# Attention heads taken in pairs: scores on both row halves of TensorE, products with V on both column halves

## What is computed

```python
def latent_attention(q, k, v, kc, vc):
    kk = jnp.concatenate([k, kc], axis=1)
    vv = jnp.concatenate([v, vc], axis=1)
    ...
    def block(qblk):
        s = jnp.einsum('bqkgd,bmkd->bkgqm', qblk, kk).astype(jnp.float32) * scale
        p = jax.nn.softmax(s, axis=-1).astype(vv.dtype)
        return jnp.einsum('bkgqm,bmkd->bqkgd', p, vv)
def token_mixer(...):
    att = latent_attention(q, k, heads(av, ATT_KV_HEADS), kc, vc)
```

## Time and profile before

| | us |
|---|---|
| time, median of 3 runs (3872.47 to 3875.03) | 3874.95 |
| the profiled execution, its own time | 3873.86 |
| its span from first to last instruction | 3872.1 |
| TensorE busy | 3644.5 (94%) |
| VectorE busy | 2787.8 (72%) |
| ScalarE busy | 2025.3 (52%) |
| granted TensorE clock, mean | 0.978 |

### The profile page before, as it was taken

One profiled execution on the slowest core, in us unless ns is written; L12 is line 12 of the kernel. 1 busy time (PEld: TensorE's weight loads), 2 busy tenths in 40 slices (PEclk: granted clock), 3 DMA queues, 4 the chain that ended last, 5 costly groups with the idle time before them and its releaser, 6 DMA issues.

```text
span 3872.1 us, 60781 instructions
## 1 busy us (share of the span) xinstructions
PE 3644.5 (94%) x22550; PEld 3149.5 (81%) x22550; DVE 2787.8 (72%) x5634; ACT 2025.3 (52%) x4198; POOL 0.2 (0%) x4
## 2 busy tenths in 40 slices
PE   7999999999997999999997999989899999969998
PEld 5876787788876899999996788878698888858887
DVE  5446744499969588888668766674765899697666
ACT  3344422466667555555557544445354666674443
POOL 0000000000000000000000000000000000000000
PEclk9999899999999999999999999999899999999999
DMA  5212223365644565556564466533044565504565
GB/s 204 80 55 99 93 88 103 109 181 183 186 150 137 153 184 185 185 185 187 186 185 131 153 190 190 175 112 106 1 148 138 176 188 181 182 1 152 185 187 159
DMA packets 142196, 568.32 MB, mean 147 GB/s; under 512 B 15808, under 2 KB 17344, under 8 KB 130240
## 3 DMA queue, kind: packets, MB, share of 16 engines
q1 hardware_dynamic: 142016, 566.16, 46.3%
HBM read 565.05 MB, written 1.05 MB: 146 GB/s over the span
## 4 chain that ended last, share of the span: by engine, by line
PE 77%; DVE 19%; ACT 2%; issue 1%; DMA 0%; SPq 0%; DVEq 0%; ACTq 0%
PE ps L530 48%; PE ps L952 12%; DVE arena L1631 11%; PE ps L970 9%; PE ps L954 6%; DVE low L1631 3%; ACT arena L1121 1%; PE ps L744 1%; DVE arena L2123 0%; DVE arena L2114 0%; DVE ring_low L1631 0%; DVE arena L2116 0%; DMA ring<-wmod_in 0%; DVE arena L2111 0%; DVE arena L2120 0%
## 5 line engine op out<-in xcount | busy, mean ns | idle before, releaser
L1121 ACT ACTIVATE high<-ring 128x512 fp32r<-128x512 f32 x1632 | 1028.5, 632 | 1026.9 <-PE ps L530 501.8
L1631 DVE TENSOR_TENSOR low<-ring,high 128x512 fp32r<-128x512 f32 x1632 | 1075.7, 688 | 286.6 <-ACT high L1121 275.8
L530 PE MATMUL ps<-h_pair,high 128*128 128x512 f32 x3456 | 1236.5, 398 | 17.4 <-DVE h_pair L1631 10.1
L530 PE MATMUL ps<-h_pair,low 128*128 128x256 f32 x3456 | 979.2, 283 | 0.0
L530 PEld LDWEIGHTS ps<-h_pair,high 128*128 128x128 f32 x3456 | 653.5, 189 | 171.1 <-issue 11.9
L952 PE MATMUL ps<-wt,high 128*128 128x512 f32 x2048 | 718.5, 397 | 5.7 <-DVE low L1631 5.7
L530 PEld LDWEIGHTS ps<-h_pair,low 128*128 128x128 f32 x3456 | 654.6, 189 | 0.0
L954 PE MATMUL ps<-wt,low 128*128 128x256 f32 x2048 | 572.0, 279 | 0.0
L530 PE MATMUL ps<-arena 128*128 128x128 f32 (+8 forms) x2456 | 408.6, 324 | 135.5 <-ACT arena L1121 109.5
L530 PEld LDWEIGHTS ps<-arena 128*128 128x128 f32 (+2 forms) x2456 | 306.6, 200 | 216.2 <-ACT arena L1121 133.3
L1121 ACT ACTIVATE arena<-ps 128x256 f32<-128x256 f32 (+2 forms) x658 | 273.1, 425 | 395.8 <-PE ps L530 352.1
(11 more groups left out here) (174 smaller groups left out, 4099.8 us busy)
## 6 DMA issues: line engine op xcount, KB each, us to landing
ring<-u_in SPq DMA_DIRECT2D x384, 512.0 KB, 3.5
ring<-v_in SPq DMA_DIRECT2D x384, 512.0 KB, 3.5
ring<-win_in SPq DMA_DIRECT2D x56, 1024.0 KB, 4.9
ring<-wmod_in SPq DMA_DIRECT2D x24, 1024.0 KB, 4.9
ring<-wq_in SPq DMA_DIRECT2D x48, 512.0 KB, 3.6
ring<-wmod_in SPq DMA_DIRECT2D x48, 512.0 KB, 3.7
ring<-wbr_in SPq DMA_DIRECT2D x16, 768.0 KB, 4.2
ring<-wout_in SPq DMA_DIRECT2D x8, 1024.0 KB, 4.9
```

Source lines behind the costliest of these rows:

```text
L530: return pe.matmul(o, l_, r, start=first, stop=last)
L1121: return act.activation(o, i_, f, **kw_)
L1631: return dve.tensor_tensor(o, a, b, op)
```

## The change

Heads are taken in the order 0, 4, 1, 5, 2, 6, 3, 7, so that neighbours in `att` lie on different row halves. TensorE issues the scores of two heads, one behind the other, and then the transposes of two heads. It runs four heads ahead instead of three (`att_p` has 4 buffers, and four scores stand ahead of the `mv` projection). In the products with V, `att_pT[part]` now holds two heads of each half (0, 1, 4, 5 and then 2, 3, 6, 7); for each block of keys there are two matmuls of 256 moving columns, one with the first 64 columns of V into partitions 0 to 63 and one with the other 64 into partitions 64 to 127. The arithmetic is the same, so is the number of scores and transposes. There are 80 matmuls with V of 256 columns in place of 40 of 512. VectorE and ScalarE keep their steps and their order in the list of heads, with each lead longer by one.

```diff
+HEADS = (0, 4, 1, 5, 2, 6, 3, 7)
...
-        att_p = view(s_mlT, 3, T)
+        att_p = view(s_mlT, 4, T)
...
-                def values(t, half):
+                def values(t, part):
...
-                    pe.wait_ge(*at("att_t_read", l, t, 4 * half + 3))
-                    part = slice(half * AD, (half + 1) * AD)
+                    pe.wait_ge(*at("att_t_read", l, t, 5 + 2 * part))
+                    two = slice(part * 2 * P, (part + 1) * 2 * P)
                     for m in range(n_m):
-                        i = mm(out_bank[t][part, :], v_tm[:, m, part],
-                               att_pT[half][:, m, :, :].rearrange("p a b -> p (a b)"), m == 0, m == n_m - 1)
-                    i.then_inc(*inc("att_pv", l, t, half))
+                        for half in range(2):
+                            hp = slice(half * AD, (half + 1) * AD)
+                            i = mm(out_bank[t][hp, two], v_tm[:, m, hp],
+                                   att_pT[part][:, m, 2 * half:2 * half + 2, :].rearrange("p a b -> p (a b)"),
+                                   m == 0, m == n_m - 1)
+                    i.then_inc(*inc("att_pv", l, t, part))
...
-                for s_ in range(3):
+                for s_ in range(4):
                     scores(*att[s_])
                 token_slot(s0 + SLOT_MV[1], "mv", 1, list(range(NT)))
-                turn_p(0, *att[0])
-                for s_, (t, h) in enumerate(att):
-                    if s_ + 3 < len(att):
-                        scores(*att[s_ + 3])
-                    if s_ + 1 < len(att):
-                        turn_p(s_ + 1, *att[s_ + 1])
+                for s_ in range(0, len(att), 2):
+                    t, h = att[s_]
+                    if s_ + 4 < len(att):
+                        scores(*att[s_ + 4])
+                        scores(*att[s_ + 5])
+                    turn_p(s_, *att[s_])
+                    turn_p(s_ + 1, *att[s_ + 1])
                     if h == 0 and t != outs(l)[0]:
                         values(t - 1, 1)
-                    if h == 4:
+                    if h == 2:
                         values(t, 0)
                 values(outs(l)[-1], 1)
...
-                    if i_ >= 3:
-                        act.wait_ge(*at("att_t", l, *att[i_ - 3]))
+                    if i_ >= 4:
+                        act.wait_ge(*at("att_t", l, *att[i_ - 4]))
...
-                    if s_ + 3 < len(att):
-                        weights(s_ + 3, *att[s_ + 3])
+                    if s_ + 4 < len(att):
+                        weights(s_ + 4, *att[s_ + 4])
                     if s_ + 1 < len(att):
                         copy_p(*att[s_ + 1])
...
+                    if s_ + 4 < len(att):
+                        smax(*att[s_ + 4])
                     if s_ + 3 < len(att):
-                        smax(*att[s_ + 3])
-                    if s_ + 2 < len(att):
-                        divide(s_ + 2, *att[s_ + 2])
+                        divide(s_ + 3, *att[s_ + 3])
```

More of the change, by code:

```diff
@@ L726, in _ @@
                 i.then_inc(*inc("cums", l))
-                att = [(t, h) for t in outs(l) for h in range(AH)]
+                att = [(t, h) for t in outs(l) for h in HEADS]
                 def scores(t, h):
@@ L743, in turn_p @@
                     for m in range(n_keys // P):
-                        i = pe.transpose(b[:, m * P:(m + 1) * P], att_p[:, i_ % 3, m * P:(m + 1) * P], ident)
+                        i = pe.transpose(b[:, m * P:(m + 1) * P], att_p[:, i_ % 4, m * P:(m + 1) * P], ident)
                     i.then_inc(*inc("att_t", l, t, h))
-                def values(t, half):
+                def values(t, part):
                     n_m = (T if t >= 2 else SEQ) // P
-                    if half == 0:
+                    if part == 0:
@@ L1321, in weights @@
                     act.wait_ge(*at("att_max", l, t, h))
-                    if i_ >= 3:
-                        act.wait_ge(*at("att_t", l, *att[i_ - 3]))
-                    fn(att_p[:, i_ % 3, 0:n_keys], b[:, 0:n_keys], ACT.Exp, scale=AD ** -0.5,
+                    if i_ >= 4:
+                        act.wait_ge(*at("att_t", l, *att[i_ - 4]))
+                    fn(att_p[:, i_ % 4, 0:n_keys], b[:, 0:n_keys], ACT.Exp, scale=AD ** -0.5,
                        bias=mx[:, t, h:h + 1], accum_out=rsum[:, t, h:h + 1]).then_inc(*inc("att_s_read", l, t, h))
-                for s_ in range(3):
+                for s_ in range(4):
                     weights(s_, *att[s_])
@@ L1342, in copy_p @@
                     n_m = (T if t >= 2 else SEQ) // P
-                    half = h // 4
+                    part, place = h % 4 // 2, h // 4 * 2 + h % 2
                     b = bank("att_t", l, t, h)
-                    if h % 4 == 0 and t != outs(l)[0]:
-                        act.wait_ge(*at("att_pv", l, t - 1, half))
-                    fn(att_pT[half][:, 0:n_m, h % 4, :], b[:, 0:n_m * P].rearrange("p (a b) -> p a b", b=P), ACT.Copy
+                    if h in (0, 2) and t != outs(l)[0]:
+                        act.wait_ge(*at("att_pv", l, t - 1, part))
+                    fn(att_pT[part][:, 0:n_m, place, :], b[:, 0:n_m * P].rearrange("p (a b) -> p a b", b=P), ACT.Copy
                        ).then_inc(*inc("att_t_read", l, t, h))
@@ L1357, in _ @@
                 for s_, (t, h) in enumerate(att):
[L1358 to L1359 removed]
+                    if s_ + 4 < len(att):
+                        weights(s_ + 4, *att[s_ + 4])
                     if s_ + 1 < len(att):
                         copy_p(*att[s_ + 1])
[L1362 removed]
+                    if h == HEADS[2] and t != outs(l)[0]:
                         copy_out(t - 1)
@@ L1816, in divide @@
                     link(dve.reciprocal(rinv[:, t, h:h + 1], rsum[:, t, h:h + 1]))
-                    dve.tensor_scalar(att_p[:, i_ % 3, 0:n_keys], att_p[:, i_ % 3, 0:n_keys], rinv[:, t, h:h + 1], None,
+                    dve.tensor_scalar(att_p[:, i_ % 4, 0:n_keys], att_p[:, i_ % 4, 0:n_keys], rinv[:, t, h:h + 1], None,
                                       ALU.mult).then_inc(*inc("att_n", l, t, h))
-                for s_ in range(3):
+                for s_ in range(4):
                     smax(*att[s_])
```

3 lines of the change are left out of this document (1 added, 2 removed).

## The result

The changed kernel takes 3837.55 us (median of four runs, 3832.38 to 3842.01), the kernel before beside it 3873.71 (3861.88 to 3875.03). The ratio is 0.991, with a 95% interval from 0.989 to 0.992. Five more executions on another occasion gave a median of 3835.3 against 3874.41, ratio 0.990 [0.988, 0.992]. The forecast of 3833 us, with a range from 3826 to 3847, holds.

What follows compares the result with a forecast made beforehand. TensorE was taken to bound the attention; savings of 24.7 us in layer 0, 14.7 in layer 1 and 1.3 ahead of them made 40.7, so 3873.9 - 40.7 = 3833 us. Range 3826 to 3847, to hold 8 in 10.

Steps and rivals of the forecast that it cites:

- The prices: TensorE's attention: 512-key score 1.10 us, paired second score free, four transposes 0.59, eight 1.03, paired products 1.00 and 1.86.
- TensorE's sum: Attention after the change: scores, transposes and products together hold TensorE 37.0 us in layer 0 and 22.3 in layer 1.
- VectorE's pace in tiles 0 and 1: Layer 0, 256 keys: a pair costs VectorE 1.96 us against TensorE's 1.72, adding 8 x 0.24 = 1.9 us.
- tight places: Attention: bank claims while `att_o` is pinned and `copy_out` ahead of an exp add 0.7 us in layer 0, 0.5 in layer 1.
- the end: End of each layer's attention: TensorE waits for the copies of the last two heads, 0.9 us each layer.
- Products not hidden: Attention: VectorE still stands idle while V is multiplied, stages 48 and 28 us, kernel 3845 us; chance 0.12.
- Overlap in part: Attention scores and products: a second tile costs a quarter of its price instead of nothing, 8 us, kernel 3841; chance 0.05.
- none: Attention pairs do not overlap at all; only ways between modes and 3 us of waits go, kernel 3863 us; chance 0.03.
- The clock: Attention falls to 1.2 GHz: over half the new stages, 3858 us, chance 0.05; over both in full, 3882 us, 0.02.
- The signs: Attention some 40 and 24 us, score pairs 0.63 and 1.1, products 1.0 and 1.86, VectorE's score waits below 12, clock 1.00.
- The sign against it: Layer 0's attention: TensorE idle ahead of transposes beyond 4 us would mean VectorE or ScalarE is the bound.
- the likeliest case: Whole kernel: 3833 us, from 3828 without added waits to 3838 with twice as many; chance 0.73.

Runs made afterwards that it cites:

- the run with the short division: Changed kernel with the division touching 2 columns of a head's weights instead of all, so the result is not computed; 3828.93 us.
- the run with the lead alone: Kernel before with four `att_p` buffers and four heads of scores ahead instead of three, all else as it was; 3867.43 us.
- the run with the early transposes: Changed kernel with `copy_out` one head earlier and, in a layer's last tile, the last pair's transposes ahead of the first products; 3835.17 us, ratio 0.990.

## Why the prediction was right

**What bounds the kernel** was read rightly: a microsecond less on TensorE in the attention was one less for the kernel, 38.7 us by the stretches and 36.2 and 39.1 by the two pairs of medians, where the prediction had 40.7.

**The prices.** The score with 512 keys was put at 1.10 from starts of weight loads and is 1.06 from starts of matmuls; the other prices hold within 0.02: 0.63 for a pair with 256 keys, 0.59 and 1.02 for four and eight transposes, 1.0 and 1.88 for the products. The pair on row halves at 512 columns, with bounds of 1.10 and 2.06, is at its lower end.

**TensorE's sum.** 37.0 and 22.3 us forecast, 38.26 and 22.41 busy. Half of what is missing in layer 0 is one pair that did not become one. The weight loads of the third pair of scores in the stretch show it:

```profile
252.44 0.29 PEld L531 LDWEIGHTS ps<-arena 64*128 64x128 f32 x2 [0.17 <-issue]
253.06 0.29 PEld L531 LDWEIGHTS ps<-arena 64*128 64x128 f32 x2 [0.32 <-ACT arena L1126]
```

The second score's load started 0.62 us behind the first's, released by ScalarE, which had still to read its bank, and the pair took 1.24 us instead of 0.63. Here the pair was none because its second wait was met too late; the prediction priced the claims as waits, not as the loss of a partner.

**What is added.** 1.9 for VectorE's pace in tiles 0 and 1, 0.7 for tight places and 0.9 at the end were 3.5 us in layer 0, against 3.95 without work. The run with the short division gives back 1.9 us in layer 0 and 0.1 in layer 1, which agrees with the first in size, but only 1.3 of them come in place, in tiles 0 and 1. The tight places were mis-sized: the claim behind `copy_out`, named as one of them, alone costs 1.16 to 1.25 us, and the prediction did not see that the change moves this copy one head back. The end is 0.64 + 0.74 = 1.38, in both layers, where 0.9 stood: the first of the two, before the last tile's first product, is new. In the kernel before no wait is listed there; two scores of its order stood ahead of that product, where the changed kernel has none left, which is the likely reason and was not tested alone. The forecast for layer 1, 23.7, was 0.3 short, that for layer 0, 40.5, 1.7.

By the rule of the Trainium skill that the emptying of PSUM may become the bound (TensorEngine Tiling (Array Packing), PSUM Bottleneck), VectorE would pace the tiles with 256 keys and, by the rows, just not the others. The runs agree in the main: with the short division layer 0 gained 1.9 us, 1.3 of them in the tiles with 256 keys, and layer 1 gained 0.1.

**The rivals.** *Products not hidden* is out: VectorE's waits fell to 8.0 us, only 1.6 of it outside the stretch of `mv`. It was a good rival, though, since in the run with the lead alone VectorE still waited 24.3 us, so the longer lead was not enough for it. *Overlap in part* and *none* are out by the prices, pair by pair. (*None* was priced with 22 pairs at 0.35 us; the stretches hold 14 + 6 = 20, and the prediction's own prices give 0.14 for the score and 0.15 for the transposes of each, so its 3863 would be some 2 us more. It decides nothing.) By the speedups of TensorE: Matmul & The Clock Gate, Measured speedup vs the span model, in the Trainium skill, which for three and four tiles are below the number of tiles, a second tile might have cost a share of the first; here two tiles did twice the work in 1.00 times the time, in rows (1.06 against 1.06) and in columns (1.88 against 1.87). *The clock* stayed at 2.4 GHz in both attentions, of the changed kernel and of its second execution. The mechanism is real all the same: it struck in the run with the early transposes, for 3.4 us and at a price of 1.5, behind a stretch in which TensorE was busy for 1.73 of 3.41 us, and in the second execution of the kernel before, at a price of 1.6, behind one with 2.82 of 3.42. That it left the two executions of the changed kernel alone is two draws and no more.

**The signs** it named came as written: attention near 40 and 24 us, pairs at 0.63 and 1.06, products at 1.0 and 1.88, waits below 12 us, and clock 1.00. The sign against it, more than 4 us of idle TensorE ahead of transposes in layer 0, did not come: the listed waits there are 1.7 + 0.2 = 1.9 us, and all its idle time is 3.95.

**The range.** 3838 as the upper end of the likeliest case covers the medians, and the range holds them, but the 2 us that it allowed for the rest of the kernel, from three runs 2.6 us apart, were too few. The executions of one kernel lay 10 to 23 us apart. In the profiled ones the stages with two durations make up most of such a spread; the others have no trace. That the medians came so near the sum is in part luck: in and ahead of the attentions the change saved 2.0 us less than forecast, and the medians lay 36.2 us apart on one occasion and 39.1 on the other.

## What to carry to other kernels

Here matmuls that use half the rows or half the columns of the array took no longer in pairs than alone, so count a change to pairs as one price per pair, and then look at what the halves wait for, since a partner that comes late is no partner. Adding up a short stretch of the trace from single prices, with the pace of the next engine beside it, gave the saving within 6%; what was missed were claims on banks at the seams between tiles, one of them made by a small move of a copy in the change itself. And an experiment that is to take an overlap away must put something between the two halves that can't overlap: changing the order of the code left most of it in place.

## What the runs showed of the chip that was not expected

- TensorE starts a matmul of the other column half while three records are still ahead of it in order. Sixteen records of two halves took 1.88 us in alternation, 1.93 in groups of four, and 2.79 in groups of eight.
- Stages of identical matmuls at the same granted clock have two durations, 491.6 or 498.8 us for the same 2836 matmuls, and which of them comes up changes from one execution to the next. Why is open; no run here was made for it.
- The same pattern of waits halved the clock in layer 0 and left it in layer 1, in one execution (TensorE busy for 1.73 of 3.41 us and 1.81 of 3.30 us). In the kernel before it fell in one execution behind 2.82 busy us of 3.42, and in the other, with the same 2.82 of 3.42 at the same place, it did not.
